# Norm and modulation as column pairs in the copies of turned rows, the router by strips, and combination weights built one block ahead

## The reference

```python
c_act = jax.nn.silu(c)
for l in range(2):
    sh1, sc1, g1, sh2, sc2, g2 = jnp.split((c_act @ w_ada[l] + b_ada[l])[:, None, :], 6, axis=-1)
    h = x * (1 + sc1) + sh1                       # modulation
    y = conformer_conv(h, ...) if l == 0 else fox_attention(h @ w_q, *shared_kv(x, c_act, ...)) @ w_o
    x = layer_norm(ALPHA * x + (1 + g1) * y, ln_mix_g[l], ln_mix_b[l])
    h = x * (1 + sc2) + sh2
    y = grouped_moe(h, router_w, router_b, w_gate[l], w_up[l], w_down[l])
    x = layer_norm(ALPHA * x + (1 + g2) * y, ln_ffn_g[l], ln_ffn_b[l])
# shared_kv: (x * (1 + scale) + shift) @ w_kvf, with a third pair of modulation rows
# grouped_moe: softmax over 16 logits, the best of 4 groups by its top two, then its top two experts
```

## Time and profile before

| | |
|---|---|
| three runs | 1451.65, 1455.3, 1455.41 us |
| profiled execution | 1454.18 us, span of its instructions 1452.4 us |
| PE busy | 1157.3 us, 80% |
| DVE busy | 411.1 us, 28% |
| ACT busy | 170.9 us, 12% |
| transfers | 494.70 MB, mean 341 GB/s over the span |

### The profile page before, as it was taken

One profiled execution on the slowest core, in us unless ns is written; L12 is line 12 of the kernel. 1 busy time (PEld: TensorE's weight loads), 2 busy tenths in 40 slices (PEclk: granted clock), 3 DMA queues, 4 the chain that ended last, 5 costly groups with the idle time before them and its releaser, 6 DMA issues.

```text
span 1452.4 us, 30514 instructions
## 1 busy us (share of the span) xinstructions
PE 1157.3 (80%) x13016; PEld 662.2 (46%) x13016; DVE 411.1 (28%) x1293; ACT 170.9 (12%) x415; POOL 21.4 (1%) x58
## 2 busy tenths in 40 slices
PE   2799978767998669867789989787689997697675
PEld 1685444433555335433374763444255553354342
DVE  0597063111222112111621331622122222121115
ACT  0003110000111001000100331010011110010001
POOL 3100000000000000000000000000000000000000
PEclk7899968888999899989879999678899998899887
DMA  9809859999999999999964022769999689999980
GB/s 374 358 20 421 357 245 398 425 425 426 366 395 410 426 427 425 422 424 424 416 273 151 24 117 92 313 268 426 423 425 396 279 353 426 427 425 422 424 347 30
DMA packets 49282, 494.70 MB, mean 341 GB/s; under 512 B 4231, under 2 KB 4247, under 8 KB 8988
## 3 DMA queue, kind: packets, MB, share of 16 engines
q1 hardware_dynamic: 48176, 490.75, 81.3%
q10 hardware_dynamic: 684, 2.32, 0.4%
q0 software_dynamic: 320, 0.16, 0.1%
HBM read 492.17 MB, written 1.05 MB: 340 GB/s over the span
## 4 chain that ended last, share of the span: by engine, by line
PE 56%; DMA 31%; DVE 8%; ACT 2%; issue 2%; ACTq 0%; DVEq 0%; POOL 0%; POOLq 0%
PE PS L904 25%; DMA ring<-in_w_up_dram 17%; DMA ring<-in_w_gate_dram 13%; PE PS L808 6%; PE PS L1011 4%; PE PS L932 3%; PE PS L742 3%; PE PS L885 2%; PE PS L826 2%; PE PS L1111 2%; DMA work<-in_conv_ln_b_dram 2%; DVE work L1381 1%; PE PS L895 1%; DVE xs L1235 1%; PE PS L792 1%
## 5 line engine op out<-in xcount | busy, mean ns | idle before, releaser
L904 PE MATMUL PS<-ring,work 128*32 128x256 f32 x8064 | 524.3, 417 | 114.6 <-DMA ring<-in_w_gate_dram 53.0
L904 PEld LDWEIGHTS PS<-ring,work 128*32 128x32 f32 x8064 | 280.2, 119 | 349.0 <-issue 110.5
L1399 DVE TENSOR_TENSOR work<-work,PS 128x256 f32<-128x256 f32 x47 | 19.8, 421 | 540.1 <-PE PS L904 540.1
L808 PE MATMUL PS<-ring,work 128*128 128x512 f32 x192 | 83.1, 593 | 0.5 <-ACT work L695 0.5
L742 PE MATMUL PS<-ring,crep 128*32 128x512 f32 x448 | 60.0, 689 | 19.7 <-DVE crep L1445 11.3
L932 PE MATMUL PS<-work 32*128 32x256 f32 x784 | 73.1, 499 | 3.1 <-ACT work L599 1.0
L904 PE MATMUL PS<-work 128*32 128x256 f32 x960 | 63.2, 408 | 15.4 <-DMA work<-in_w_up_dram 15.4
L922 PE MATMUL PS<-ident,work 128*128 128x128 f32 x94 | 22.9, 329 | 64.1 <-DVE work L1385 64.1
L1480 DVE SCALAR_TENSOR_TENSOR work<-work,colv 128x256 f32<-128x256 f32 x150 | 64.2, 486 | 1.2
L885 PE MATMUL PS<-hs,work 128*32 128x256 f32 x784 | 56.3, 406 | 3.8 <-DVE work L1372 3.8
L808 PEld LDWEIGHTS PS<-ring,work 128*128 128x128 f32 x192 | 36.3, 190 | 46.1 <-issue 45.3
(11 more groups left out here) (220 smaller groups left out, 884.9 us busy)
## 6 DMA issues: line engine op xcount, KB each, us to landing
ring<-in_w_gate_dram SPq DMA_DIRECT2D x64, 2048.0 KB, 26.2
ring<-in_w_up_dram SPq DMA_DIRECT2D x54, 2048.0 KB, 26.2
ring<-in_w_down_dram SPq DMA_DIRECT2D x54, 2048.0 KB, 27.9
ring<-in_w_ada_dram SPq DMA_DIRECT2D x24, 2048.0 KB, 18.8
work<-in_w_up_dram SPq DMA_DIRECT2D x10, 2048.0 KB, 23.9
work<-in_w_down_dram SPq DMA_DIRECT2D x10, 2048.0 KB, 27.4
ring<-in_w_pw_dram SPq DMA_DIRECT2D x6, 2048.0 KB, 38.8
ring<-in_w_ada_kv_dram SPq DMA_DIRECT2D x4, 2048.0 KB, 15.1
```

The source lines that it names most:

```text
L808: last = pe.matmul(PS[:, banks + 2 * t + q, :], rows[:, k, t * P:(t + 1) * P], quarter(index + h, kk, KH)[:, q * BANK:(q + 1) * BANK], sta ...
L904: last = pe.matmul(dst[SLOTS * s:SLOTS * (s + 1), :], rows[:, cc, SLOTS * q:SLOTS * (q + 1)], quarter(load + h, kk, KH)[:, QUART * s:QUART ...
```

## The change

1. **The norm in the copies.** After the root, `hs` holds the plain normalized rows: half on VectorE, half on ScalarE (`n_half`). TensorE turns them at once (`turn_n`). The norm's gain and offset and the modulation's scale and shift are applied as two columns (`scale`, `shift`, one number per feature, which is one per partition after turning) in the copies out of PSUM (`copy_hT`). The columns come from `columns` (8 matmuls with four columns each), `copy_cols` on ScalarE, and `affine` on GpSimd, which multiplies gain and scale. The kernel's input is turned unmodulated at the start.
2. **The full rows later.** `xs` with gain and offset is still needed for the residual; `keep_x` makes it after `take_xT` of the mixture, or during the keys' projection.
3. **Modulation groups without a wait.** `ada` for the next group goes to bank 6 and no longer waits for `y_read`; `crep` is gone (the weights are `cact` broadcast).
4. **The router by strips.** 8 matmuls of 256 columns with `rw` as weights, four side by side, two copies (`parts`), and 4 small matmuls that add the strips. `ranks` is 5 operations on all pairs.
5. **The mixture.** `take_xT` multiplies and adds the columns (two operations for one), the sums are zeroed by ScalarE, and `build_GW(n + 1)` runs at the end of block n. The down matmuls wait for `XT_copied` too.
6. **The start.** Small loads on ACT's queue change places: the rows for the convolution first, the biases after `silu`, four new ones with the norms' rows (`lnr_in`) near the end. The spread of the taps stands inside the first projection, at f == 2.

The diff, cut to its core:

```diff
-            def copy_hT():
+            def copy_hT(scale, shift, ready=None):          # DVE; ACT alike with Identity, scale and bias
+                if ready is not None:
+                    dve.wait_ge(acol_ready, ready)
                 for b in (1, 3):
                     dve.wait_ge(h_turned, 4 * turned[0] + b + 1)
-                    dve.tensor_copy(hT[:, 2 * b:2 * b + 2, :],
-                                    PS[:, b, :].rearrange("p (k t) -> p k t", k=2)).then_inc(hT_copied, 1)
+                    for k in (2 * b, 2 * b + 1):
+                        last = dve.tensor_scalar(hT[:, k, :], PS[:, b, (k % 2) * SEQ:(k % 2 + 1) * SEQ],
+                                                 scale[:, k:k + 1], shift[:, k:k + 1], ALU.mult, ALU.add)
+                    last.then_inc(hT_copied, 1)
...
                 link(dve.reciprocal(rstd[:, :], rstd[:, :]))
+                if done is None:
+                    dve.scalar_tensor_tensor(out=negm[:, 0:1], in0=mv[:, 1, 0:1], scalar=-1.0, in1=rstd[:, 1:2],
+                                             op0=ALU.mult, op1=ALU.mult).then_inc(shift_ready, 1)
+                    dve.tensor_scalar(chunks(hs, 0), by_chunk(xs[:, 0, :]), mv[:, 0, 0:1], rstd[:, 0:1],
+                                      ALU.subtract, ALU.mult).then_inc(h_ready, 1)
+                    if ada_next is not None:
+                        add_ada(*ada_next, 6)
+                    return
...
+                    act.wait_ge(shift_ready, norms[0] // TT)
+                    act.activation(chunks(hs, 1), by_chunk(xs[:, 1, :]), ACT.Identity, bias=negm[:, 0:1],
+                                   scale=rstd[:, 1:2]).then_inc(n_half, 1)
...
+            def keep_x(banks):
+                x_of = lambda t: by_chunk(xs[:, t, :])
+                with_row(banks[0], x_of, lambda t: chunks(hs, t), ALU.mult)
+                with_row(banks[1], x_of, x_of, ALU.add)
...
+            def affine(to, gain, offset, scale, shift):      # POOL
+                pool.tensor_tensor(acol[:, to, 0, :], lncol[:, :, gain], mcol[:, scale[0], scale[1], :], ALU.mult).then_inc(acol_part, 1)
+                pool.tensor_tensor(acol[:, to, 1, :], lncol[:, :, offset], mcol[:, scale[0], scale[1], :], ALU.mult).then_inc(acol_part, 1)
...
             def moe(index, l):
-                for t in range(TT):
-                    for k in range(KD):
-                        last = pe.matmul(PS[:, B_GATE, t * E:(t + 1) * E], hT[:, k, t * P:(t + 1) * P],
-                                         rw[:, k, :], start=(k == 0), stop=(k == KD - 1))
+                h_there()
+                for kk in range(2):
+                    for q in range(4):
+                        last = pe.matmul(PS[32 * q:32 * q + 32, (B_GATE, B_M)[kk], 0:SEQ],
+                                         rw[:, 2 * q:2 * q + 2, :].rearrange("p k e -> p (k e)"), hT[:, 2 * q + kk, :],
+                                         start=True, stop=True, tile_position=(0, 32 * q), skip_group_check=True)
+                    last.then_inc(logits_parted, 1)
...
-            norm_spreads(1, 0, L_ADA1_G2)
+            spread_mod(modv[1], 2, 4)
+            ada(L_ADA1_G2, 6)
             pe.wait_ge(ada_added, 7)
-            spread_mod(modv[1], 4)
-            spread_mod(modv[1], 3)
-            turn_h()
+            columns(7, ((modv[1], 1), (modv[1], 2)))
+            turn_n(3)
             moe(L_MOE1, 1)
...
                 def take_xT(n):
-                    dve.tensor_copy(XT.rearrange("p c s -> p (c s)"), XT_ps).then_inc(XT_copied, 1)
+                    dve.tensor_tensor(to, XT_ps.rearrange("p (c q s) -> p c q s", c=NC, q=STRIPS), over[0], ALU.mult).then_inc(XT_begun, 1)
+                    dve.wait_ge(XT_begun, n + l)
+                    dve.tensor_tensor(to, to, over[1], ALU.add).then_inc(XT_copied, 1)
...
                 def result_of(n):                            # DVE
-                    build_GW(n)
                     for i in range(2):
                         last = dve.tensor_scalar(late[i][:, :], late[i][:, :], float(SLOTS), None, ALU.subtract)
...
                     dve.tensor_copy(GWT, GWT_ps).then_inc(GWT_copied, 1)
+                    dve.wait_ge(late_on, n)
+                    build_GW(n + 1)
```

More of the change, by code:

```diff
@@ L451, in _ @@
             pool.memset(ahead[:, :, :], float(SLOTS)).then_inc(consts, 1)
-            for v in range(PER):
-                last = pool.memset(later[:, :, v:v + 1], float(PER - 1 - v))
-            last.then_inc(consts, 1)
-            pool.wait_ge(consts, 12)
+            pool.memset(lower[:, :, :], 1.0).then_inc(consts, 1)
+            pool.wait_ge(consts, 11)
             pool.affine_select(out=ident[:, :], in_=ident[:, :], compare_op=ALU.not_equal, fill=1.0, base=0,
@@ L573, in layer_norm_root @@
                     act.activation(dst, y, ACT.Copy).then_inc(y_read, 1)
+                if groups is not None:
+                    copy_cols(7, groups)
                 for t in range(TT):
@@ L602, in moe @@
                 take_x(act.snap(n_act) + 1)
+                act.wait_ge(spread_used, (3, 9)[l])
+                for b in range(4):
+                    act.activation(PS[:, b, :], ones[:, 0:1].to_broadcast([P, BANK]), ACT.Copy,
+                                   scale=0.0).then_inc(sums_zeroed, 1)
                 for e in range(E):
@@ L766, in spread_row @@
                     r, v = row(i)
-                    last = pe.matmul(PS[:, 4 + 2 * (n % 2) + i, :], ones[r:r + 1, :], v, start=True, stop=True)
+                    last = pe.matmul(PS[:, bank + i, :], ones[r:r + 1, :], v, start=True, stop=True)
                     if i == 0:
@@ L771, in spread_row, with columns, spread_mod @@
                 spreads[0] += 1
-            def spread_mod(tile, v):
+            def columns(bank, tiles):
+                for i, (tile, g) in enumerate(tiles):
+                    for j in range(4):
+                        at = 16 * i + 4 * j
+                        last = pe.matmul(PS[:, bank, at:at + 4], tile[:, g, j:BANK:4], ident[:, 0:P:32],
+                                         start=True, stop=True, skip_group_check=True)
+                        if i == j == 0:
+                            behind(last)
+                last.then_inc(col_done, 1)
+            def spread_mod(tile, v, bank):
                 def row(i):
@@ L876, in moe @@
                 if l == 0:
-                    zero_sums()
                     pe.wait_ge(ada_added, 5)
@@ L983, in _ @@
+            columns(5, ((modv[0], 0),))
             pe.wait_ge(colrows_in, COLROWS)
             for k in range(KD):
-                last = pe.transpose(PS[:, B_Y, k * 40:k * 40 + NROWS], colrows[0:NROWS, k * P:(k + 1) * P],
-                                    ident[0:NROWS, 0:NROWS])
-            last.then_inc(cols_turned, 1)
-            pe.wait_ge(cols_copied, 1)
-            for q in range(4):
-                for s in range(4):
-                    of_shift = colv[:, :, s:TAPS:4]
-                    last = pe.matmul(PS[32 * s:32 * s + 32, 1, 64 * q:64 * (q + 1)].rearrange("p (k m) -> p k m", k=KD)[:, :, 0:of_shift.shape[2]],
-                                     ident[:, 32 * q:32 * q + 32], of_shift, start=True, stop=True,
-                                     tile_position=(0, 32 * s), skip_group_check=True)
@@ L1053, in _ @@
                     pe.wait_ge(conv_ready, KD)
-                last = pe.matmul(PS[:, 4, 0:SEQ], ones_d[:, :], CV[:, k, :], start=(k == 0), stop=(k == KD - 1))
+                last = pe.matmul(PS[:, 4, 0:SEQ], ones[:, :], CV[:, k, :], start=(k == 0), stop=(k == KD - 1))
                 if k == 0:
```

362 lines of the change are left out of this document (218 added, 144 removed).

## The result

The changed kernel takes 1417.2 us (median of 4 runs, 1413.0 to 1420.5) against 1455.4 before (1451.7 to 1458.3): a ratio of 0.975, 95% interval 0.971 to 0.978. The forecast was 1412, range 1399 to 1430. The profiled execution took 1419.2 us, its span 1417.4, 35.0 less than before.

A forecast was written before the change was run, and what follows sets the result against it. It took the weights' stream as the limit in the mixtures, and TensorE's way to freeing loads outside them. Terms 2.6 - 14.3 - 3.2 - 11.5 - 12.1 - 5.0 = -43.5 from 1455.3 gave 1411.8, said as 1412 us, range 1399 to 1430.

The forecast's parts named there:

- +2.6, bounds 0 and +5: Start of the kernel: first projection ends at 110.6 us against 108.3, plus 0.3 for sigmoids; 2.6 us lost.
- with 0.3 for later sigmoids: Part of the start's term: later sigmoids behind the first projection cost 0.3 us.
- -14.3 on load 30: Ahead of layer 0's mixture: norm, turn, router and modulation changes let load 30 leave 14.3 us earlier, before the start's loss.
- -12.0: Norm ahead of layer 0's mixture: 14.2 us from reciprocal's end to first transpose become 2.15, 12.0 us less.
- -3.2 and -5.0: Mixtures of layers 0 and 1: weights built a block ahead remove a 2.0 us wait; 3.2 and 5.0 us less.
- for a single block the change gives nothing: Mixtures: a block takes TensorE 16.0 us against 29.6 for an expert's six loads, so one-block experts gain nothing.
- The cap that I drew from the stream's losses: Mixtures: the gain cannot exceed what the stream lost, 11 us in layer 0 and 26 in layer 1.
- -11.5: Keys' projection: earlier, shorter turn and two spreads gone, less norm rows and extra copies; 11.5 us less.
- -12.1: Ahead of layer 1's mixture: TensorE's path counts whole, with norm, turn, router and ranks shorter; 12.1 us less.
- The start comes late: Rival: late small loads start the first projection 20 us late, 1433 us; with others that eat gain, chance 0.15.
- The strided half: Rival: the norm's strided half costs 0.8 us, not 1.95, and the clock stays up, 1400 us; chance 0.11.
- The slower case: Rival: in the mixtures `take_xT` and the `XT_copied` wait cost 1.1 us in each of 47 blocks, 1464 us; chance 0.04.

The follow-up runs named there:

- with the sigmoids first: Changed kernel with ScalarE's two copies of the spread taps moved behind the sigmoids of f = 0 and f = 1: 1408.9 us, ratio 0.970.
- with the taps first: Changed kernel with TensorE spreading the taps ahead of the first projection (f = 0) instead of at f = 2: 1402.9 us, ratio 0.966; a second set 1406.0 us, 0.969.
- The router put back: Changed kernel with taps spread at f = 0, and the router's logits by 16 matmuls as before instead of strips: 1409.5 us, ratio 0.970.
- The part alone: Kernel before with only the combination weights built one block ahead and the wait for copied rows ahead of the down projection: 1430.3 us, ratio 0.985.
- the weights put back: Changed kernel with the combination weights built in the block's own turn again, the rest kept: 1441.3 us, ratio 0.992.

## Why the prediction was near, and where it was wrong

*The start, "+2.6, bounds 0 and +5": wrong, 11.0.* What I worked out on TensorE was near. Its first matmuls ran at the lower level (granted clock 0.50 from 48 to 52), and the first projection ended at 112.46 where I had 110.6. Behind its wait for the load it ran at the lower level once more (0.50 from 58 to 60), and its next 52 matmuls took 13.17 us against 11.49 with the sigmoids first. With ScalarE's order mended it ends at 110.45 and the mean is 2.3 us late, and with the taps first 1.1. The step that failed is "with 0.3 for later sigmoids". It priced a copy by its length, not by what it waits for and what stands behind it on ScalarE: the taps' copies wait for f = 2, two pieces of 6.9 us into the projection, and eight sigmoids with 70 us of VectorE's work queue behind them. The prediction counted SyncE's and TensorE's order and not ScalarE's. It cost 8.7 us at the mean.

*Before layer 0's mixture, "-14.3 on load 30": -12.8.* Load 30 left at 216.56 (218.34 before), with the mean 11.0 later. By load 31's landing it is -10.1. The prediction let load 30 alone decide, and said that load 29 costs nothing unless it passes 207; it left at 212.48, and loads 26 to 31 landed with one pause of 0.8 us, so load 26, 15.2 us late, set the pace. For load 30 itself the sum is near, its first term is not. "-12.0" for the norm assumed that the turn follows it, 2.15 us behind the reciprocal's end; it stands 4.0 behind it, where it stood 14.2, and the gain is 10.1. The turn waits behind the modulation group, which itself stands behind the columns; the columns took 3.90 us at the lower clock, and I had priced none in this stage. The turn gave 1.2 for my 0.8 and the router 4.3 for my 3.1, which makes up for most of it. The router put back costs 2.5 at load 31.

*In the mixtures, "-3.2 and -5.0": too small.* The mechanism was right, the size wrong: -6.4, and -9.9 with the end. The part alone gives 8.4 and 14.0 there. Its landings show where. Away from the experts with several blocks, the last loads of two experts in a row land 29.5 us apart in both kernels, so "for a single block the change gives nothing" holds for the stream. The gain comes around the runs of 3, 2, 2 and of 3, 2, 3 blocks: by the last load of the ninth expert it is 7.3 and 11.3 us, where I had 2.1 and 3.5. What failed is the price: 1.6 us for an expert left out the combination's slower matmuls, 0.5 each, and half of layer 0's run was taken off for loads in store. Three experts at 2.0 and 0.5 us are 7.6, near layer 0's 7.3; why layer 1 gains 11.3 stays open. The cap that I drew from the stream's losses (11 us in layer 0) held.

*The keys, "-11.5": -9.9* (the output projection starts at 859.14 against 874.47, with 5.4 of the 15.3 brought along). The keys' projection itself is 13.1 earlier relative to the mixture's end, near the -13.8 predicted, though the turn gained 9.8 us behind the reciprocal where I had 11.3. The rows in the middle took the 2.0 that I had for them, but the projection's own matmuls were 2.4 shorter (28.2 against 30.5). What was lost lies at the first query, where the turned rows are copied with their scale:

```profile
784.13 0.39 PE L1212 MATMUL PS<-ident,work 16*128 16x16 f32 x2 [2.56 <-DVE work L1330]
784.45 6.71 PE L1222 MATMUL PS<-work,ring 128*128 128x256 f32 x16
```

These 16 matmuls took 3.72 us before, behind a wait of 1.94. Here they ran largely at the lower level (granted clock 0.59 from 784 to 792), which cost 3.0 us; the wait is 0.6 longer. That the longer wait brought the clock down isn't shown: behind the same 2.56 the other runs took 5.09 to 6.72, and the kernel with the weights alone took 5.39 behind 1.95.

*Before layer 1's mixture, "-12.1": -10.1* (926.79 against 952.17, less the 15.3): from the reciprocal's end to the turn it is 8.7 less, and norm, columns and sum together had 8.5. The sum behind VectorE's half costs 2.0 in the wait, and 3.3 with what follows, where I had 0.75, so this agreement is luck in part. The 2 us are missing behind it, where the clock was at the lower level: the way from the turn to the router became 0.65 us longer, where I had 0.8 less, and the router gave 0.7 for my 1.5.

*The rivals.* "The start comes late" was right in kind, 8.4 more than my term, by another road. The strided half was neither of the two prices (below). The slower case did not come; its mechanism, the second operation on the rows, is real, but worth some 3 to 7 us in all. The signs that I had named came out accordingly: the keys' projection starts 18.5 us earlier and not 29, layer 1's strips 25.4 and not 38.5. So the sum was near partly by luck: errors of both signs met in it. Measured less predicted: start +8.4, from there to load 31 +4.2, mixtures and end -8.0, between the mixtures +3.9, together 8.5 us, which is the span of 1417.4 less the 1408.9 that the sum gave for it. Not taken out alone, and so not told apart, are the norm in the copies, the groups without a wait, the shorter `ranks` and the sums zeroed by ScalarE; what is said of them is read from the waits.

## What to carry to other kernels

When a step moves, follow it on every engine that has a piece of it, and ask what stands behind that piece in that engine's order: a copy of 0.4 us that waits for a later producer is as long as the wait. A short wait that recurs costs its own length and the slower work right behind it; sum both over all its places before you call it hidden, and look for the places where the other limit has no slack to give: here the runs of experts with several blocks. When two limits stand close together, as load 26 and load 30 here, moving one of them gives little. And when two things end close together ahead of a step, as the norm and the modulation group here, take the later one's end as the step's start before you price a gain on the other.

## What the runs showed of the hardware that was not expected

- **A single GpSimd operation of 0.79 us took 5.92 us.** In the changed kernel the third tap stack (four operations, 127.00 to 135.18) begins beside VectorE's taps with two inputs in SBUF, 14 of them without a break; in the runs with the sigmoids first or the taps first the same four take 3.02 and 3.05:

```profile
127.00 8.18 POOL L523 TENSOR_TENSOR hs<-lane,work 128x256 f32<-128x256 f32 x4 [50.39 <-PE PS L1147]
```

```profile
125.00 3.02 POOL L523 TENSOR_TENSOR hs<-lane,work 128x256 f32<-128x256 f32 x4 [49.59 <-PE PS L1148]
```

  It came again with the weights put back (8.2 us) and in none of the other ten profiles (3.02 to 3.06), so it goes with the program. The Trainium skill (SBUF — State Buffer, SBUF: two separate sides) says that an operation of VectorE with two SBUF inputs and one of GpSimd that reads SBUF exclude each other for a whole instruction. The short operations agree: beside each of them one of VectorE's takes 0.72 us, where their mean is 0.488. What goes with the long case is VectorE's pace. In both kernels that have it, VectorE's operations (0.48 us each) start every 0.40 us, each before the one ahead has ended, until a first pause of 0.04 us (at 132.45 here), and GpSimd's operation ends 0.5 us behind that pause. In the ten others they start every 0.52 us, or every 0.75 beside GpSimd's, with such a pause ahead of each. That GpSimd gets in only at a pause is the reading that fits; no run tests it.
- **The strided half.** VectorE's half of the norm, 1024 elements read by `by_chunk`, took 1.25 us: neither the 1.95 that I took from a sum of two tensors nor the 0.8 of the contiguous form, for which the rule that I weighed spoke. ScalarE's half, the same read, took 2.33, while its copy of as many elements from PSUM without a stride takes 0.97 (two in 1.94 at 191.44); the source and the function differ too, so that the stride is the cause isn't shown.
